# A Fourier table of 129 cosine and 127 sine columns, and key transposes ahead of a gate half, in a two-block transformer kernel

## What is computed

```python
def fourier_mix(u):                       # u: 256 tokens x 512, as 4 groups of 128
    ug = u.reshape(b, s, FOURIER_GROUPS, FOURIER_GROUP_DIM).astype(jnp.float32)
    f = jnp.fft.fft2(ug, axes=(1, 3), norm="ortho").real
    return f.reshape(b, s, FOURIER_WIDTH).astype(u.dtype)

z = h @ w_in[l]
u_f, q_lat, kv_lat, k_rope, gate_logits = jnp.split(z, [SPLIT_1, SPLIT_2, SPLIT_3, SPLIT_4], axis=-1)
y_a = fourier_mix(u_f) @ w_fourier_out[l]
y_b = mla_attention(q_lat, kv_lat, k_rope, positions, q_norm[l], w_q_up[l],
                    kv_norm[l], w_kv_up[l]) @ w_mla_out[l]
gate_a, gate_b = jnp.split(jax.nn.sigmoid(gate_logits), 2, axis=-1)
y = (gate_a * y_a + gate_b * y_b) @ w_out[l]
```

## Time and profile before

| | |
|---|---|
| time, median of 3 runs | 1138.01 us (1137.35 to 1138.54) |
| the profiled execution, its own time | 1138.07 us |
| its span, first to last instruction | 1136.3 us |
| PE busy | 1097.5 us, 97% of the span |
| DVE busy | 855.4 us, 75% |
| ACT busy | 552.0 us, 49% |
| POOL busy | 47.2 us, 4% |
| granted PE clock, mean | 0.993 of full speed |
| read from HBM | 263.60 MB, 234 GB/s over the span |

### The profile page before, as it was taken

One profiled execution on the slowest core, in us unless ns is written; L12 is line 12 of the kernel. 1 busy time (PEld: TensorE's weight loads), 2 busy tenths in 40 slices (PEclk: granted clock), 3 DMA queues, 4 the chain that ended last, 5 costly groups with the idle time before them and its releaser, 6 DMA issues.

```text
span 1136.3 us, 16194 instructions
## 1 busy us (share of the span) xinstructions
PE 1097.5 (97%) x6084; PEld 942.6 (83%) x6084; DVE 855.4 (75%) x909; ACT 552.0 (49%) x664; POOL 47.2 (4%) x78
## 2 busy tenths in 40 slices
PE   7799999999999999999999999999999999999996
PEld 5698887879988788888979888888788888888886
DVE  4888898775967778878868988877764787666664
ACT  3244444453576654444464444446444446444442
POOL 1000000010121100000010000001000000000001
PEclk9999999998999999999999999999999999999999
DMA  8899997636431589987669999745553355667641
GB/s 323 324 383 369 352 358 282 226 120 220 149 112 59 176 306 322 306 310 259 202 227 331 353 367 332 252 142 171 172 187 110 121 176 182 225 213 232 220 168 56
DMA packets 144981, 266.91 MB, mean 235 GB/s; under 512 B 9657, under 2 KB 103974, under 8 KB 139686
## 3 DMA queue, kind: packets, MB, share of 16 engines
q1 hardware_dynamic: 143040, 262.96, 66.6%
q0 software_dynamic: 1056, 3.17, 0.9%
q10 hardware_dynamic: 838, 0.15, 0.1%
HBM read 263.60 MB, written 2.65 MB: 234 GB/s over the span
## 4 chain that ended last, share of the span: by engine, by line
PE 76%; DVE 9%; ACT 5%; issue 4%; DMA 4%; SPq 1%; POOL 1%; DVEq 0%; ACTq 0%; POOLq 0%
PE ps L1787 17%; PE ps L1724 11%; PE ps L1726 11%; PE ps L1725 11%; PE ps L1789 8%; PE ps L1768 4%; PE ps L1770 4%; PE ps L1771 4%; DVE w_lo L1111 3%; DMA arena<-in_w_ada 2%; DVE arena L1190 2%; DMA w_raw<-in_w_ada 2%; ACT w_hi L760 1%; DVE nT L1335 1%; ACT nT_both L760 1%
## 5 line engine op out<-in xcount | busy, mean ns | idle before, releaser
L1111 DVE TENSOR_TENSOR w_lo<-w_raw,w_hi 128x2048 fp32r<-128x2048 f32 (+3 forms) x170 | 383.2, 2258 | 108.3 <-ACT w_hi L760 107.6
L760 ACT ACTIVATE w_hi<-w_raw 128x2048 fp32r<-128x2048 f32 (+3 forms) x170 | 319.3, 1885 | 253.6 <-PE ps L1726 115.1
L1787 PE MATMUL ps<-nT_both,w_hi 128*128 128x512 f32 x1024 | 363.1, 399 | 2.7 <-DVE h_act L1217 2.7
L1789 PE MATMUL ps<-nT_both,w_lo 128*128 128x256 f32 x1024 | 287.4, 281 | 0.0
L1787 PEld LDWEIGHTS ps<-nT_both,w_hi 128*128 128x128 f32 x1024 | 192.4, 188 | 52.1 <-DVE h_act L1217 4.8
L1789 PEld LDWEIGHTS ps<-nT_both,w_lo 128*128 128x128 f32 x1024 | 193.3, 189 | 1.0
L1190 DVE SCALAR_TENSOR_TENSOR arena<-arena,c_act 128x3072 f32<-128x3072 f32 (+2 forms) x49 | 129.9, 2650 | 2.1 <-DMA arena<-in_w_ada 1.3
L1724 PE MATMUL ps<-w_hi,hT_hi 128*128 128x512 f32 x328 | 128.7, 392 | 0.0
L1726 PE MATMUL ps<-w_hi,hT_lo 128*128 128x512 f32 x328 | 128.1, 390 | 0.0
L1725 PE MATMUL ps<-w_lo,hT_hi 128*128 128x512 f32 x328 | 127.9, 390 | 0.0
L1768 PE MATMUL ps<-nT_both,w_hi 128*128 128x256 f32 x416 | 120.0, 289 | 0.0
(11 more groups left out here) (266 smaller groups left out, 1236.9 us busy)
## 6 DMA issues: line engine op xcount, KB each, us to landing
arena<-in_w_ada SPq DMA_DIRECT2D x16, 1536.0 KB, 9.4
arena<-in_ada_w SPq DMA_DIRECT2D x16, 1536.0 KB, 8.2
w_raw<-in_w_in SPq DMA_DIRECT2D x46, 512.0 KB, 4.6
w_raw<-in_w_ffn_down SPq DMA_DIRECT2D x44, 512.0 KB, 4.3
w_raw<-in_ffn_w_down SPq DMA_DIRECT2D x44, 512.0 KB, 4.1
w_raw<-in_w_ffn_gate SPq DMA_DIRECT2D x42, 512.0 KB, 6.1
w_raw<-in_w_ffn_up SPq DMA_DIRECT2D x42, 512.0 KB, 7.2
w_raw<-in_ffn_w_gate SPq DMA_DIRECT2D x42, 512.0 KB, 4.1
```

Of the source, the lines that this page charges most:

```text
L760: copy = lambda o, i: act.activation(o, i, ACT.Copy)
L1111: dve.tensor_tensor(lo(s, n), raw(s, n), hi(s, n).bitcast(F32), ALU.subtract).then_inc(lo_ready[s], 1)
L1787: pe.matmul(ps[:, i, :], hi(s)[:, cols], nT_both[:, kk].rearrange("p a n -> p (a n)"), start=(kk == 0), stop=False, skip_group_check=True)
L1789: last = pe.matmul(ps[:, i, 0:S], lo(s)[:, cols], nT_hi[:, kk, :], start=False, stop=(kk == KD - 1), skip_group_check=True)
```

## The change

The table over the tokens keeps 129 cosine columns (0 to 128) and 127 sine columns (1 to 127) in place of 256 and 256, since cosine columns n and 256 - n are equal and sine columns n and 256 - n are each other's negative. Step one has matmuls of 256 columns. Step two no longer adds in PSUM: the cosine part goes to 129 columns and the sine part to 127 columns beside them. DVE copies the sine parts out (`sin_part`, L1621 of the changed kernel), copies columns 0 and 128 (L1622), writes cosine plus sine to columns 1 to 127 (L1624) and cosine less sine, backwards, to columns 255 to 129 (L1625). `f_out` is then waited for at 3.

Of the 32 transposes the 16 of the keys stay behind `g2 0`, and the 16 of the queries stand behind `g2 1`. The copies to `kT` are ahead of the rounding of `g3 1` on ACT, and on DVE ahead of `fr_lo`; those to `qT` stay where they were.

```diff
-        dft = carve(5120, 2, NB)
+        dft = carve(5120, 2, S)
-        cu = carve(6400, 4, NB)
+        cu = carve(6400, 4, S)
+        sin_part = carve(7424, 4, S - COS)
...
# ACT
-                copy(cu[:, g, :], ps[:, 4 + g, :]).then_inc(cu_out, 1)
+                copy(cu[:, g, :], ps[:, 4 + g, 0:S]).then_inc(cu_out, 1)
...
             hi2("g3 0")
-            act.wait_ge(f_out, 4)
+            act.wait_ge(f_out, 3)
             copy(fr_hi, nT[:, 4:8, :]).then_inc(f_hi, 1)
+            def qkT_evict(dst, first):
+                for i in range(first, first + 4, 2):
+                    act.wait_ge(qk_tr, i + 1)
+                    copy(dst[0:QH, 2 * (i % 4):2 * (i % 4) + 2, :], ...).then_inc(qkT_out, 1)
+            qkT_evict(kT, 0)
             hi2("g3 1")
-            for i in range(0, 8, 2):
-                act.wait_ge(qk_tr, i + 1)
...
+            qkT_evict(qT, 4)
             hi2("fourier 0")
...
# DVE
             dve.wait_ge(f_mm, 1)
-            for g in range(4):
-                dve.tensor_copy(nT[:, 4 + g, :], ps[:, 4 + g // 2, (g % 2) * S:(g % 2 + 1) * S]).then_inc(f_out, 1)
+            f_cols = ps[:, 4:6, :].rearrange("p b (g n) -> p (b g) n", n=S)
+            dve.tensor_copy(sin_part, f_cols[:, :, COS:S]).then_inc(f_sin, 1)
+            dve.tensor_copy(nT[:, 4:8, 0:COS:COS - 1], f_cols[:, :, 0:COS:COS - 1]).then_inc(f_out, 1)
+            dve.wait_ge(f_sin, 1)
+            dve.tensor_tensor(nT[:, 4:8, 1:COS - 1], f_cols[:, :, 1:COS - 1], sin_part, ALU.add).then_inc(f_out, 1)
+            dve.tensor_tensor(nT[:, 4:8, S - 1:COS - 1:-1], f_cols[:, :, 1:COS - 1], sin_part, ALU.subtract).then_inc(f_out, 1)
             lo2("g3 0")
+            qkT_evict(kT, 0)
             dve.wait_ge(f_hi, 1)
             dve.tensor_tensor(fr_lo, nT[:, 4:8, :], fr_hi.bitcast(F32), ALU.subtract).then_inc(f_lo, 1)
-            for i in range(1, 8, 2):
...
+            qkT_evict(qT, 4)
             lo2("g3 1")
...
# PE
-                    last = pe.matmul(ps[:, 4 + g, :], uf[:, k, g * P:(g + 1) * P], dft[:, k, :], start=(k == 0), stop=(k == 1))
+                    last = pe.matmul(ps[:, 4 + g, 0:S], uf[:, k, g * P:(g + 1) * P], dft[:, k, :], start=(k == 0), stop=(k == 1))
...
-                pe.matmul(o, dftd[:, 0, :], cu[:, g, 0:S], start=True, stop=False, skip_group_check=True)
-                last = pe.matmul(o, dftd[:, 1, :], cu[:, g, S:2 * S], start=False, stop=True, skip_group_check=True)
+                pe.matmul(o[:, 0:COS], dftd[:, 0, :], cu[:, g, 0:COS], start=True, stop=True, skip_group_check=True)
+                last = pe.matmul(o[:, COS:S], dftd[:, 1, :], cu[:, g, COS:S], start=True, stop=True, skip_group_check=True)
             last.then_inc(f_mm, 1)
             pe.wait_ge(grp_out, 22)
             half2("g2 0", NB, (2, 3))
-            pe.wait_ge(f_out, 4)
-            for i in range(8):
...
+            pe.wait_ge(f_out, 3)
+            qk_transposes(0)
             half2("g2 1", NB, (2, 3))
+            qk_transposes(4)
             pe.wait_ge(grp_out, 24)
             half2("g3 0", NB, (0, 1))
```

More of the change, by code:

```diff
@@ L41 @@
 QL, KVL = 384, 256
+COS = S // 2 + 1
 def program(nc, a, out):
@@ L230, in program @@
         q_scaled = sem("q_scaled")
-        dft_loaded, cu_mm, cu_out, f_mm, f_out, f_hi, f_lo = map(
-            sem, ["dft_loaded", "cu_mm", "cu_out", "f_mm", "f_out", "f_hi", "f_lo"])
+        dft_loaded, cu_mm, cu_out, f_mm, f_sin, f_out, f_hi, f_lo = map(
+            sem, ["dft_loaded", "cu_mm", "cu_out", "f_mm", "f_sin", "f_out", "f_hi", "f_lo"])
         trig_arg, trig_done, trig_ready = map(sem, ["trig_arg", "trig_done", "trig_ready"])
@@ L1051, in _ @@
             hi2("g3 0")
-            act.wait_ge(f_out, 4)
+            act.wait_ge(f_out, 3)
             copy(fr_hi, nT[:, 4:8, :]).then_inc(f_hi, 1)
-            hi2("g3 1")
-            for i in range(0, 8, 2):
-                act.wait_ge(qk_tr, i + 1)
-                dst = kT if i < 4 else qT
-                copy(dst[0:QH, 2 * (i % 4):2 * (i % 4) + 2, :],
-                     ps[0:QH, 4 + i % 4, :].rearrange("p (k n) -> p k n", n=S)).then_inc(qkT_out, 1)
+            def qkT_evict(dst, first):
+                for i in range(first, first + 4, 2):
+                    act.wait_ge(qk_tr, i + 1)
+                    copy(dst[0:QH, 2 * (i % 4):2 * (i % 4) + 2, :],
+                         ps[0:QH, 4 + i % 4, :].rearrange("p (k n) -> p k n", n=S)).then_inc(qkT_out, 1)
+            qkT_evict(kT, 0)
+            hi2("g3 1")
+            qkT_evict(qT, 4)
             hi2("fourier 0")
@@ L1614, in _, with qkT_evict @@
             dve.wait_ge(f_mm, 1)
-            for g in range(4):
-                dve.tensor_copy(nT[:, 4 + g, :], ps[:, 4 + g // 2, (g % 2) * S:(g % 2 + 1) * S]).then_inc(f_out, 1)
-            lo2("g3 0")
+            f_cols = ps[:, 4:6, :].rearrange("p b (g n) -> p (b g) n", n=S)
[4 more added lines that the diff above has]
+            dve.tensor_tensor(nT[:, 4:8, S - 1:COS - 1:-1], f_cols[:, :, 1:COS - 1], sin_part, ALU.subtract).then_inc(f_out, 1)
+            lo2("g3 0")
+            def qkT_evict(dst, first):
+                for i in range(first + 1, first + 4, 2):
+                    dve.wait_ge(qk_tr, i + 1)
+                    dve.tensor_copy(dst[0:QH, 2 * (i % 4):2 * (i % 4) + 2, :],
+                                    ps[0:QH, 4 + i % 4, :].rearrange("p (k n) -> p k n", n=S)).then_inc(qkT_odd, 1)
+            qkT_evict(kT, 0)
             dve.wait_ge(f_hi, 1)
             dve.tensor_tensor(fr_lo, nT[:, 4:8, :], fr_hi.bitcast(F32), ALU.subtract).then_inc(f_lo, 1)
-            for i in range(1, 8, 2):
[L1621 to L1624, removed]
+            qkT_evict(qT, 4)
             lo2("g3 1")
@@ L2158, in _, with qk_transposes @@
             half2("g2 0", NB, (2, 3))
-            pe.wait_ge(f_out, 4)
-            for i in range(8):
[L2162 to L2172, removed]
+            def qk_transposes(first):
+                pe.wait_ge(qk_ready, first // 4 + 1)
+                for i in range(first, first + 4):
+                    src = k_row if i < 4 else q_row
+                    if i >= 4:
+                        pe.wait_ge(qkT_odd if i % 2 else qkT_out, i // 2 - 1)
+                    for j in range(2):
+                        h = 2 * (i % 4) + j
+                        for t in range(T):
+                            last = pe.transpose(ps[0:QH, 4 + i % 4, j * S + t * P:j * S + (t + 1) * P],
+                                                src[:, t, h * QH:(h + 1) * QH], ident[:])
+                    last.then_inc(qk_tr, 1)
+            pe.wait_ge(f_out, 3)
+            qk_transposes(0)
             half2("g2 1", NB, (2, 3))
+            qk_transposes(4)
             pe.wait_ge(grp_out, 24)
@@ L2300, in dft_tables @@
     wd = 2 * np.pi * ((d[:, None] * d[None, :]) % P) / P
-    over_s = np.concatenate([np.cos(ws), np.sin(ws)], 1) / np.sqrt(S)
+    over_s = np.concatenate([np.cos(ws)[:, 0:COS], np.sin(ws)[:, 1:COS - 1]], 1) / np.sqrt(S)
     over_d = np.concatenate([np.cos(wd), -np.sin(wd)], 1) / np.sqrt(P)
```

## The result

| | before | after |
|---|---|---|
| median of 5 runs, same chip | 1137.38 us (1135.38 to 1138.54) | 1130.49 us (1128.57 to 1131.54) |
| ratio | | 0.9937, 95% interval 0.9923 to 0.9952 |
| the profiled execution, its own time | 1138.07 | 1129.26 |
| its span | 1136.3 | 1127.5 |
| granted PE clock, mean | 0.993 | 0.997 |

The kernel became faster by 0.6%, between 5.5 and 8.8 us. The forecast was 5.8 us less and a time of 1132.3, in a range from 1131.0 to 1134.6; the median lies 0.5 us under that range. So the direction and the size of the change were about right, and the absolute time and its range were wrong. The two profiled executions even differ by 8.8 us, 3 more than forecast, and the first question is where that lies.

What follows compares the result with a forecast made beforehand. PE was taken to bound the kernel, holding 76% of the chain of waits. Savings of 3.42 + 1.69 + 0.70 = 5.81 us took 1138.07 to 1132.3, own range 1131.4 to 1133.2, with rivals 1131.0 to 1134.6.

Steps and rivals of the forecast that it cites:

- Step one: Eight PE matmuls, 256 columns in place of 512: 6.87 us should become 3.45, saving 3.42.
- Step two: Eight PE matmuls of 129 and 127 columns: 3.45 us should become 1.76, saving 1.69.
- Rival A: Weight loads bound the matmuls of 129 and 127 columns: 3.07 us there, gain 4.50, time 1133.6; chance 0.05.
- The copies out of PSUM: DVE's copies and sums behind step two end 1.2 us before PE finishes `g2 0`, and cost nothing.
- Rivals B and C: DVE's backward sum is slow: sums four times as long, 1135.2, chance 0.03; eight times, 1140.8, chance 0.03.
- The transposes: 32 on PE around `g2 0` and `g2 1`: PE's 0.70 us wait for ACT's key copy goes, saving 0.70.
- The sum: Savings of step one, step two and the transposes together: 3.42 + 1.69 + 0.70 = 5.81 us.
- rival E: Nothing arrives at the end, since a later load or split sets the pace: 1138.1; chance 0.02.
- D: Granted clock falls once more, at the border from M2 to F3, losing 5.1 us: 1137.4; chance 0.05.
- The absolute time: Whole kernel: from the profiled execution's 1138.07 us down to 1132.3, 0.5% less.

Runs made afterwards that it cites:

- the plain kernels: Kernel before and changed kernel, both without the widening of M1's index-key matmuls from 72 columns; medians over all runs 1136.89 and 1130.50 us.
- the second one of before: Kernel before, unchanged, profiled once more; that one execution took 1139.09 us.
- the tables alone: Changed kernel with 256-column index-key matmuls, but transposes and copies in the order of before on all three engines; 1130.99 us.

## Why the prediction was right and where it was wrong

**Step one** was right: 3.42 us forecast, 6.87 to 3.45 measured. Everything that had to be ready earlier was: PE has no new wait.

**Step two** was right: 1.69 forecast, 3.45 - 1.79 = 1.66 measured. The row with 128 columns was the right one. 16 instructions took 1.79 us, 56 ns for each of 32 passes if they are two apiece. The 81 ns a pass that the prediction took from the Trainium skill ("TensorE: Matmul & The Clock Gate", section Back-to-back issue gap), an estimate of 2.59 us for the step, is too slow for this case. Rival A fell.

**The copies out of PSUM** were right: cover forecast 1.2, measured 1.4 to 1.5. It is longer because DVE's next operation starts 0.09 before the one ahead of it ends (841.52 against 840.92 + 0.69), so that 0.69 counts as 0.60. Rivals B and C fell: the backward sum took 0.68.

**The transposes** were mis-sized: 0.70 forecast, 1.04 measured (4.54 to 2 x 1.75), 1.02 when done alone. The mechanism was right. The step that failed is "the last 16 took 1.92; the first 16 the same": the 1.92 held about 0.17 for the start after the wait. That was counted as the transposes' own time, in both halves, and so in what was left after the change. Without it the first 16 end at 854.00, and PE waits 0.87, not 0.70; 0.87 and 0.17 are the 1.04. The 0.89 us that PE is idle in the earlier trace rows, which the prediction itself puts down to this wait, would have given 0.9.

**The sum** was 5.81 against 6.09 to 6.10 between the marks; nearly all of the difference is the transposes. Nothing was given back behind the scores; rival E fell, and so did D at the place where it was put.

**The absolute time** is where the prediction failed, in two sentences. "The profiled execution took 1138.07 in all, so 1132.3" started from an execution with a long fall of the clock, which cost 3.1 us there. The rows of that fall were in hand and stood in rival D as a price (5.1 us, where the marks show 3.1), but were taken as a fixed part of the kernel. They are a draw: from 3.4 to 10.3 us at 1.2 GHz in the five profiles of the plain kernels. And "the 0.6 us by which the runs of before spread" took the spread of 3 runs (1.2 us) for that of the kernel; 54 runs span 4.5. From their median, 1136.89, the forecast of 5.8 gives 1131.1, and the measured 6.1 gives 1130.8, beside 1130.50 for 16 runs of the changed kernel. The 0.8 us by which the first comparison (6.89) goes beyond 6.1 is no more than such draws can do to medians of five, and its interval, 5.5 to 8.8, holds 6.1. So of the 1.8 us between 1132.3 and 1130.49, 0.7 is the base (1138.07 against a median of 1137.38), 0.3 the change itself, and 0.8 the draw of the changed kernel's five runs.

**Rival D** had the wrong cause, too. It blamed the pause at the border. The regular fall began 3.3 to 6.0 us behind the first of the narrow matmuls, in three of the five profiles among them and in two up to 0.8 us behind the last, and it went away when they were made wider with the pause unchanged. Whether the narrow matmuls would bring it without the pause some 13 us ahead of them was not tested. Falls behind a pause came as well, but not each time: at the border from F0 to M1 in 2 of 13 profiles (the second one of before, and 128 columns), at the border from M1 to F1 in 1 of 13 (the tables alone), and behind the wait of 2.9 us in the one profile of the sums done four times. The Trainium skill ("TensorE: Matmul & The Clock Gate", section Part 1: The HAM clock gate) says of a kernel's first matmuls that the window in which the chip watches PE's activity is free-running, so that the number of matmuls at the slow clock differs from run to run. The profiles show the like for this later fall: 3.4, 6.8 and 3.4 us for one kernel. Had such a draw been weighed, the range would have had to reach down by the 3.1 us that the fall of before cost.

## What to carry to other kernels

Read the granted clock of the profile before taking its time as the base of a forecast: a fall in it can be a draw, and then belongs in the range on both sides, however far from the change it lies. Its price is not half its length: read it between two marks around it. To measure a change of a few microseconds, read the chain between two marks around it, or first take the fall away in both kernels; that gave 6.09 and 6.10 in two pairs where the medians of five runs gave 6.9. A matmul row that begins behind a wait holds the start as well: take an instruction's price from a row without a wait in front of it.

## What was not expected of the hardware

With 48 matmuls of 72 columns, issued without a pause, one every 0.111 us, the clock fell to 1.2 GHz in all five profiles of the plain kernels, among them or just behind. With 128 or 256 columns, one every 0.111 and 0.12 us, it stayed at 2.4 GHz there in all eight profiles. So the wider matmuls cost 0.01 us each or nothing, and steady issue alone did not keep the clock. Widths between 72 and 128 were not tried.
